# The pool band of a hybrid decoder trunk: the rows of the tile above, packed by a DMA for two matmuls instead of eight

## The chip, the cores and the metric

One core of one Trainium2 chip runs the whole program. The metric is the device time of one execution in microseconds (us); for the kernel before there are three such times, and their median is used. The profile is of one execution.

## The reference, cut to what matters

Two layers over 1024 positions of 1024 channels in float32. The first mixes tokens by trailing means over 2, 4, 8 or 16 positions (one window for each group of 256 channels), minus the token itself, followed by a 256x256 product in each group; the second is a sliding-window attention. Each layer then has a SwiGLU part and an embedding part.

```
hn = rms_norm(h, mix_pre_g[i])
for g, w in enumerate((2, 4, 8, 16)):
    pooled[g] = (cs[t] - cs[t - w]) / min(t + 1, w) - hn[g]       # cs: cumulative sum over positions
y = einsum('bsgc,gcd->bsgd', pooled, w_pool) * pool_scale
h = h + rms_norm(y, mix_post_g[i])
h = h + rms_norm(swiglu(rms_norm(h, ffn_pre_g[i])), ffn_post_g[i])
```

## The kernel before, in words

The 1024 positions are eight tiles of 128. The normed tile t lies in `pool_xn[t % 2]` with its positions on the partitions. `pool_band` turns a tile and takes its trailing means at once: for each of the eight blocks of 128 channels it multiplies the block by a constant band matrix (`band_inner`, L631). The first positions of a tile also need up to 15 positions of the tile above, so behind each of these eight matmuls comes one with 16 columns, which reads the block of the tile above in `pool_xn[1 - p]` and the constant `band_before` (L633). All are float32, and each shows as two MATMUL records. The result fills PSUM banks 0 and 1, which there are only once: the next band waits until ScalarE has taken the high part (`slot_hi`, L395) and VectorE the low part (`slot_lo`, L399).

Each engine runs a list of parts in written order (`staggered`). In step t the parts are these. TensorE: band(t+1), the turn of tile t-2 for the SwiGLU part (`fn_turn`, L517), products(t) (24 matmuls, L315 to L317). VectorE: `add_post(t-1)` (L472 and L475, adds the tile's output to H), `pool_normed(t+2)` (L371), `slot_lo(t+1)` (L399), `fn_normed(t-1)` (L506), `fn_lo(t-2)` (L552). ScalarE: `slot_hi(t+1)`, the squares of tile t+3 (L645), the raw copies of tile t-2 (L533), the squares of H for tile t-1 (L492), the squares of products(t) (L594), the cuts of tile t-2 (L543). GpSimd turns sums of squares into scales (L364, L366; L498, L500). Products(t) go to banks 2+3 or 4+5 by parity. `pool_normed(t+2)` writes the buffer of tile t, and so waits until band(t+1), which still reads it, has ended.

The SyncE queue issues loads in written order: the eight tiles of x, the constants, the pool weights, `sinks`, and then in `ffn_loads(0)` three weight loads of the SwiGLU part (A11, A12, A21), followed by `spill_tile(0..4)`, each of which waits for `add_post` of its tile (`added`). Behind them are the other weight loads. The semaphores of the p loads are four, one for each layer and parity.

Of the kernel before, what the change touches and what calls it, by code (L numbers as in the profile page):

```python
# [22 lines left out]
P = 128  # L23
F32 = mybir.dt.float32
# [6 lines left out]
D = 1024  # L31
SEQ = 1024
TILES = SEQ // P
PAIRS = TILES // 2
KD = D // P
HALF = 512
# [5 lines left out]
LONGEST = max(WINDOWS)  # L42
# [14 lines left out]
def constants():  # L57

    s, t = np.arange(P)[:, None], np.arange(P)[None, :]
    first, inner, before = [], [], []  # L60
    for w in WINDOWS:
        near = (t >= s) & (t - s < w)
        first.append(near / np.minimum(t + 1, w).astype(np.float32) - (s == t))
        inner.append(near / np.float32(w) - (s == t))
        before.append(((t + P - s < w) / np.float32(w))[:, :LONGEST])
    inv = (1.0 / (10000.0 ** (np.arange(0, HEAD, 2, dtype=np.float32) / np.float32(HEAD)))).astype(np.float32)
    angle = np.arange(SEQ, dtype=np.float32)[:, None] * inv[None, :]
    angle = angle.reshape(TILES, P, HEAD // 2).transpose(1, 0, 2)
    q, k = np.arange(P)[:, None], np.arange(-P, P)[None, :]
    valid = (q - k >= 0) & (q - k < P)  # L70
    mask = np.stack([np.where(valid & (k >= 0), 0.0, NEG), np.where(valid, 0.0, NEG)], axis=1)
    out = {
        "identity": np.eye(P),
        "band_first": np.stack(first, 1), "band_inner": np.stack(inner, 1), "band_before": np.stack(before, 1),
        "rope_cos": np.cos(angle), "rope_sin": np.sin(angle),
        "mask_unit": np.concatenate([mask[:, 0], mask[:, 1], np.zeros((P, D - 4 * P))], axis=1),
    }
    return {k: np.ascontiguousarray(v, dtype=np.float32) for k, v in out.items()}
# [12 lines left out]
def trunk(nc, I, out):  # L91
    ctx = ExitStack()
    with ctx:
        credited = []

        def sem(name):
            return ctx.enter_context(nc.semaphore(name))
# [54 lines left out]
        def at(kib, *tensors):  # L152
# [8 lines left out]
        Z = region("Z", 186 * KIB,  # L161

                   at(0, *[(f"raw{i}", [P, D], F32) for i in range(SLOTS)], ("xn0", [P, D], F32), ("xn1", [P, D], F32),
                      ("tmp", [P, D], F32)),

                   at(0, ("b11_hi", PIECES, F32R), ("b11_lo", PIECES, F32R), ("t3_lo", PIECES, F32R)),
                   at(16, ("t3_raw", PIECES, F32)),
                   at(24, ("a11_hi", FORM, F32R), ("a11_lo", FORM, F32R), ("a12_hi", FORM, F32R), ("a12_lo", FORM, F32R),
                      ("m7", [P, HALF], F32), ("d_s4_hi", [P, 2 * P], F32R), ("d_s4_lo", [P, 2 * P], F32R),
# [22 lines left out]
                   at(96, ("late_junk", [P, D], F32)), at(28, ("ffn_junk", [P, D], F32)),  # L192

                   at(36, *weights("w_pool", [P, KD, GROUP]), ("band_first", [P, 4, P], F32), ("band_inner", [P, 4, P], F32),
                      ("band_before", [P, 4, LONGEST], F32), ("scale_row", [P, D], F32), ("pool_gain", [P, D], F32),
                      ("squares", [P, 2, D], F32), ("pool_xn0", [P, D], F32), ("pool_xn1", [P, D], F32),
                      ("pool_raw0", [P, D], F32), ("pool_raw1", [P, D], F32)),
                   at(92, ("pool_junk", [P, 2, D], F32)),
# [18 lines left out]
        A = B = DD = E = Z  # L217
        raw = [Z[f"raw{i}"] for i in range(SLOTS)]
        pool_raw, pool_xn = [Z["pool_raw0"], Z["pool_raw1"]], [Z["pool_xn0"], Z["pool_xn1"]]
        xn, tmp = [Z["xn0"], Z["xn1"]], Z["tmp"]  # L220
        xt_hi, xt_lo = [DD["xt0_hi"], DD["xt1_hi"]], [DD["xt0_lo"], DD["xt1_lo"]]
        post_gain = E["post_gain"]
# [17 lines left out]
        ps = ctx.enter_context(nc.psum_tensor("ps", [P, 8, HALF], F32))  # L240
# [79 lines left out]
        consts_loaded = sem("consts_loaded")  # L320
        first_consts_loaded = sem("first_consts_loaded")
        pool_consts_loaded = sem("pool_consts_loaded")
        w_pool_scaled = sem("w_pool_scaled")
        x_loaded = [sem(f"x_loaded{t}") for t in range(TILES)]
        gain_loaded = sem("gain_loaded")
# [17 lines left out]
        def moved(count):  # L343
            return 16 + 32 * count

        p_loaded = [[sem(f"p_loaded{L}{p}") for p in range(2)] for L in range(2)]
        stored = sem("stored")


# [269 lines left out]
        def pool_band(pe, i, p):  # L619

            s = s_pool
            first = isinstance(i, int) and i == 0 and p == 0
            if isinstance(i, int) and i == 0 and p == 1:
                pe.wait_ge(pool_consts_loaded, 48)
            pe.wait_ge(s["xn"][p], s.done("xn", i))
            t_banks_read(pe, s, i, p)
            for c in range(KD):
                w = c // 2
                band = B["band_first"] if first else B["band_inner"]
                o = banks(0)[:, c * P:(c + 1) * P]  # L630
                last = pe.matmul(o, pool_xn[p][:, c * P:(c + 1) * P], band[:, w, :], start=True, stop=first)  # L631
                if not first:
                    last = pe.matmul(o[:, 0:LONGEST], pool_xn[1 - p][:, c * P:(c + 1) * P], B["band_before"][:, w, :],  # L633
                                     start=False, stop=True)
            last.then_inc(s["turned"][p], 1)
            if first:

                for w in range(12):
                    pe.matmul(ps[:, 6, 0:P], B["band_first"][:, w % 4, :], B["band_first"][:, w % 4, :], start=True, stop=True)
# [143 lines left out]
        def ffn_load(sp, name, source, L, g, t):  # L783

            w = I["w_ff_gate" if source[1] == "1" else "w_ff_up"][L].rearrange("(k p) n -> p k n", p=P)
            k = 4 * (int(source[2]) - 1)
            sp.dma_start(W_RAW[name][:, :, :], w[:, k:k + 4, bass.ds(g * GROUP + t * P, P)]
                         ).then_inc(F["form_loaded"][name], 16)
# [668 lines left out]
        def p_load(sp, L, i, p):  # L1457
            s = S[f"ple{L}"]
            sp.wait_ge(s["p_lo"][p], s.free("p_lo", i))
            sp.dma_start(p_raw[p][:, :, :], I["pT"][L].rearrange("(k c) t -> c k t", c=P)[:, :, bass.ds((2 * i + p) * P, P)]  # L1460
                         ).then_inc(p_loaded[L][p], 16)

        def p_hi(act, L, i, p):
            s = S[f"ple{L}"]
            act.wait_ge(p_loaded[L][p], 16 * i + 16)
            act.wait_ge(s["used"][p], s.free("used", i))
            act.activation(pT[p][0][:, :, :], p_raw[p][:, :, :], ACT.Copy).then_inc(s["p_hi"][p], 1)

# [322 lines left out]
        def _(sp):  # L1791
# [6 lines left out]
            sp.dma_start(B["band_first"][:, :, :], I["band_first"]).then_inc(first_consts_loaded, 16)  # L1798
            w = I["pool_w"][0].rearrange("g c n -> (g c) n")
            x_load(1)  # L1800
            for name in ("band_inner", "band_before"):
                sp.dma_start(B[name][:, :, :], I[name]).then_inc(pool_consts_loaded, 16)
            sp.dma_start(ident[:, :], I["identity"]).then_inc(pool_consts_loaded, 16)
            row_load(sp, B["scale_row"], I["pool_scale"][0], pool_raw_loaded[0])
# [3 lines left out]
            for t in range(3, TILES):  # L1808
                x_load(t)
            sp.dma_start(sinks[:, :], I["sinks"][0].partition_broadcast(P)).then_inc(consts_loaded, 16)  # L1810

            def ffn_loads(L):
                s = S[("pool", "o")[L]]

                def spill_tile(j):
                    sp.wait_ge(s["added"][j % 2], s.done("added", j // 2))
                    sp.dma_start(spill[L][:, j * D:(j + 1) * D], H[:, j * D:(j + 1) * D]).then_inc(F["spilled"], 16)

                first = (0, 0)
                if L == 1:  # L1820
                    sp.wait_ge(s["used"][0], s.done("used", 0))
                ffn_load(sp, "A11", "a11", L, *first)
                ffn_load(sp, "A12", "a12", L, *first)
                if L == 1:
                    sp.wait_ge(*summed("S4", 0, GROUPS - 1, 1))
                ffn_load(sp, "A21", "a21", L, *first)
                for j in range(5):
                    spill_tile(j)
                if L == 1:
                    sp.wait_ge(s["lo"][0], s.done("lo", PAIRS - 1))  # L1830
                ffn_load(sp, "S2", "a22", L, *first)
                sp.wait_ge(s["used"][0], s.done("used", PAIRS - 1))
                ffn_load(sp, "S3", "a11", L, *first)
                ffn_load(sp, "S1", "a22", L, *first)
                spill_tile(5)
                spill_tile(6)
                sp.wait_ge(FN["ssum"], done(TILES * L + TILES - 1))
                ffn_load(sp, "A22", "a22", L, *first)
                spill_tile(TILES - 1)
                ffn_load(sp, "S4", "a12", L, *first)  # L1840
                ffn_load_down(sp, L, 0)
                for t in range(2):
                    ffn_load_tile(sp, L, 0, t)
                with sp.Fori(1, GROUPS - 1) as g:
                    for t in range(2):
                        ffn_load_tile(sp, L, g, t)
                for t in range(2):
                    ffn_load_tile(sp, L, GROUPS - 1, t)
# [601 lines left out]
```

## Time and profile before

| | |
|---|---|
| time of three executions | 1977.02, 1977.14, 1977.79 us; median 1977.14 us |
| span of the profiled execution | 1974.5 us; its own time isn't given apart, the median is 2.6 us above the span |
| TensorE matmul busy | 1923.7 us (97%) |
| VectorE busy | 1410.7 us (71%) |
| ScalarE busy | 897.2 us (45%) |
| GpSimd busy | 457.6 us (23%) |
| the chain that ended last | PE 86%, DVE 8%, POOL 2%, issue 2% |
| pool stage | band(0) starts at 9.64 us, band(7) at 65.55 us, its last products at 74 to 77 us |

In the profile PE is TensorE's matmuls, DVE is VectorE, ACT ScalarE, POOL GpSimd, SPq the queue of SyncE. PEclk is the granted share of TensorE's full clock. A row of a timeline gives start, duration, engine, line, operation, tiles written and read, and in brackets the idle time before it.

### The profile page before, as it was taken

How to read it: one execution, taken by the hardware profiler on the slowest of the kernel's cores; microseconds unless marked ns; L12 is line 12 of the kernel's file. 1: busy time of each engine (PE TensorE's matmuls, PEld its weight loads, DVE VectorE, ACT ScalarE, POOL GpSimd, SP SyncE). 2: the span in 40 equal slices, each digit the busy share in tenths (PEclk: the TensorE clock that was granted, in tenths of full speed). 3: DMA queues.
4: the chain of work that ended last, by engine and by line, in shares of the span. 5: the costliest groups of instructions: out<-in, count | busy, mean ns of one | idle time of the engine just before them, and what ended most of it. 6: DMA issues, size and time to landing. Idle time of an engine off the chain costs nothing.

```text
span 1974.5 us, 28696 instructions
## 1 busy us (share of the span) xinstructions
PE 1923.7 (97%) x9198; PEld 1578.6 (80%) x9198; DVE 1410.7 (71%) x2384; ACT 897.2 (45%) x1726; POOL 457.6 (23%) x448
## 2 busy tenths in 40 slices
PE   7899999999999999999999999999999999999998
PEld 7778888888888878888866687888888888888787
DVE  6887777777777786565478658777777777777863
ACT  5654444444444454341178545444444444444531
POOL 3211222212122221010046211222122221222310
PEclk9999999999999999999999999999999999999999
DMA  5333323233333350254200113233332323235201
GB/s 210 107 97 96 92 82 97 75 102 94 98 94 92 89 203 24 78 221 168 85 12 1 60 48 114 79 101 96 96 95 86 90 74 106 90 105 178 96 29 68
DMA packets 221159, 189.02 MB, mean 96 GB/s; under 512 B 11168, under 2 KB 198944, under 8 KB 221088
## 3 DMA queue, kind: packets, MB, share of 16 engines
q1 hardware_dynamic: 217712, 183.38, 29.0%
q10 hardware_dynamic: 3376, 4.73, 0.7%
q8 instruction: 40, 0.66, 0.1%
q14 instruction: 31, 0.25, 0.0%
HBM read 167.10 MB, written 20.97 MB: 95 GB/s over the span
## 4 chain that ended last, share of the span: by engine, by line
PE 86%; DVE 8%; POOL 2%; issue 2%; ACT 1%; DMA 1%; DVEq 0%; ACTq 0%; POOLq 0%
PE ps L825 14%; PE ps L827 14%; PE ps L826 14%; PE ps L315 7%; PE ps L317 7%; PE ps L316 7%; PE ps L922 7%; PE ps L924 7%; PE ps L923 7%; POOL probs L1679 1%; DVE ps L1644 1%; PE ps L388 1%; PE ps L1633 1%; PE ps L1687 1%; PE ps L631 1%
## 5 line engine op out<-in xcount | busy, mean ns | idle before, releaser
L1247 DVE TENSOR_TENSOR H<-H,ps 128x512 f32<-128x512 f32 x496 | 327.9, 686 | 112.9 <-PE ps L924 112.0
L1109 POOL TENSOR_TENSOR s_raw<-s_raw,a_raw 128x512 f32<-128x512 f32 x66 | 87.5, 1327 | 765.6 <-DVE s_lo L1160 649.3
L825 PE MATMUL ps<-t_hi,s_hi 128*128 128x512 f32 x528 | 206.3, 391 | 6.8 <-DVE t_lo L1259 3.9
L827 PE MATMUL ps<-t_hi,s_lo 128*128 128x512 f32 x528 | 205.5, 389 | 0.0
L826 PE MATMUL ps<-t_lo,s_hi 128*128 128x512 f32 x528 | 205.5, 389 | 0.0
L998 ACT ACTIVATE m<-ps 128x512 f32<-128x512 f32 x44 | 26.4, 599 | 264.9 <-PE ps L827 262.6
L825 PE MATMUL ps<-b_hi,a_hi 128*128 128x512 f32 x352 | 137.7, 391 | 0.0
L826 PE MATMUL ps<-b_lo,a_hi 128*128 128x512 f32 x352 | 137.5, 391 | 0.0
L827 PE MATMUL ps<-b_hi,a_lo 128*128 128x512 f32 x352 | 137.4, 390 | 0.0
L924 PE MATMUL ps<-wd_hi,d_ab_lo 128*128 128x512 f32 x336 | 130.7, 389 | 0.0
L922 PE MATMUL ps<-wd_hi,d_ab_hi 128*128 128x512 f32 x336 | 130.7, 389 | 0.0
L923 PE MATMUL ps<-wd_lo,d_ab_hi 128*128 128x512 f32 x336 | 130.7, 389 | 0.0
L825 PEld LDWEIGHTS ps<-t_hi,s_hi 128*128 128x128 f32 x528 | 99.1, 188 | 29.9 <-DVE t_lo L1259 5.3
L827 PEld LDWEIGHTS ps<-t_hi,s_lo 128*128 128x128 f32 x528 | 99.1, 188 | 20.8
L826 PEld LDWEIGHTS ps<-t_lo,s_hi 128*128 128x128 f32 x528 | 99.1, 188 | 20.4
L976 ACT ACTIVATE s_hi<-s_raw 128x512 fp32r<-128x512 f32 x132 | 82.8, 627 | 54.8 <-DVE s_raw L1109 54.8
L1160 POOL TENSOR_TENSOR a_lo<-a_raw,a_hi 128x512 fp32r<-128x512 f32 x60 | 80.9, 1348 | 114.7 <-ACT a_hi L976 114.7
L315 PE MATMUL ps<-w_ple_gate_hi,xt_hi 128*128 128x512 f32 x256 | 101.7, 397 | 1.6 <-DVE w_ple_gate_lo L291 0.8
L317 PE MATMUL ps<-w_ple_gate_hi,xt_lo 128*128 128x512 f32 x256 | 100.0, 390 | 0.0
L316 PE MATMUL ps<-w_ple_gate_lo,xt_hi 128*128 128x512 f32 x256 | 99.6, 389 | 0.0
L1679 POOL TENSOR_TENSOR probs<-probs,recip 128x1024 f32<-128x1024 f32 x32 | 60.6, 1893 | 153.3 <-DVE recip L1671 153.3
L939 ACT ACTIVATE ps<-ps 128x512 f32<-128x512 f32 x88 | 51.2, 582 | 98.0 <-PE ps L924 90.8
(293 smaller groups left out, 5033.6 us busy)
## 6 DMA issues: line engine op xcount, KB each, us to landing
a_raw<-in_w_ff_gate SPq DMA_DIRECT2D x88, 256.0 KB, 2.9
a_raw<-in_w_ff_up SPq DMA_DIRECT2D x88, 256.0 KB, 3.0
s_raw<-in_w_ff_up SPq DMA_DIRECT2D x88, 256.0 KB, 2.9
s_raw<-in_w_ff_gate SPq DMA_DIRECT2D x88, 256.0 KB, 3.1
wd_raw<-in_w_ff_down SPq DMA_DIRECT2D x44, 512.0 KB, 4.3
residual_spill<-H SPq DMA_DIRECT2D x16, 512.0 KB, 2.6
raw<-in_w_ple_gate SPq DMA_DIRECT2D x16, 512.0 KB, 6.0
back<-residual_spill SPq DMA_DIRECT2D x16, 512.0 KB, 5.3
```

The lines of the kernel that those rows point to most:

```text
L315: pe.matmul(out_, lhs[0], rhs[0], start=first, stop=False)
L316: pe.matmul(out_, lhs[0], rhs[1], start=False, stop=False)
L317: return pe.matmul(out_, lhs[1], rhs[0], start=False, stop=last)
L825: pe.matmul(ps[:, bank, :], w[0], x[0], start=fresh and k == 0, stop=False, skip_group_check=not fresh)
L826: pe.matmul(ps[:, bank, :], w[0], x[1], start=False, stop=False, skip_group_check=not fresh)
L827: last = pe.matmul(ps[:, bank, :], w[1], x[0], start=False, stop=k == 3, skip_group_check=not fresh)
L922: pe.matmul(ps[:, bank, :], a[0], wd_hi[:, b, :], start=fresh, stop=False, skip_group_check=not fresh)
L923: pe.matmul(ps[:, bank, :], a[0], wd_lo[:, b, :], start=False, stop=False, skip_group_check=not fresh)
L924: pe.matmul(ps[:, bank, :], a[1], wd_hi[:, b, :], start=False, stop=True, skip_group_check=not fresh).then_inc(F["down"], 1)
L976: act.activation(W[name][0][:, :, :], form_raw(name), ACT.Copy).then_inc(F["form_hi"], 1)
L1109: eng.tensor_tensor(form_raw(name), W_RAW[name][:, :, :], form_raw(other) if other != "A21" else W_RAW["A21"][:, :, :], op).then_inc(summe ...
L1247: dve.tensor_tensor(dst, dst, src, ALU.add).then_inc(F["summed"], 1)
```

## The change: what it does

The eight matmuls of 16 columns go. Instead SyncE copies the last sixteen rows of each normed tile (16 partitions of 1024 values) into a tile `halo[t % 2]` of 128 partitions by 128 values: row r, channel block c lands on partition 8r + c. A constant `band_halo`, of two blocks of 64 columns, picks from it by channel block, so two matmuls of 64 columns (one for each bank) add all eight corrections. They stand behind the eight inner matmuls and wait for the copy. The copies of tiles 0, 1 and 2 stand in the SyncE queue behind the load A21, the copy of tile j+3 behind the spill of tile j. The semaphores of the p loads become two, with counts that run on over the layers; `band_before` (32 KB) gives way to `band_halo` (64 KB).

```diff
+    halo = np.zeros((P, 2, HALF // KD), np.float32)
+    for c in range(KD):
+        at_ = (c % 4) * LONGEST
+        halo[c::KD, c // 4, at_:at_ + LONGEST] = before[c // 2]
...
-                last = pe.matmul(o, pool_xn[p][:, c * P:(c + 1) * P], band[:, w, :], start=True, stop=first)
-                if not first:
-                    last = pe.matmul(o[:, 0:LONGEST], pool_xn[1 - p][:, c * P:(c + 1) * P], B["band_before"][:, w, :],
-                                     start=False, stop=True)
+                last = pe.matmul(o, pool_xn[p][:, c * P:(c + 1) * P], band[:, w, :], start=first or c % 4 == 0, stop=True,
+                                 skip_group_check=not first and c % 4 > 0)
+            if not first:
+                pe.wait_ge(halo_loaded[1 - p], 16 * (i + p))
+                for b in range(2):
+                    o = ps[:, b, :].rearrange("p (c t) -> p c t", c=4)[:, :, 0:LONGEST]
+                    last = pe.matmul(o, halo[1 - p][:, :], B["band_halo"][:, b, :].rearrange("p (c t) -> p c t", c=4),
+                                     start=False, stop=True, skip_group_check=True)
             last.then_inc(s["turned"][p], 1)
...
-            act.wait_ge(p_loaded[L][p], 16 * i + 16)
+            act.wait_ge(p_loaded[p], 16 * (L * PAIRS + i) + 16)
...
+            def halo_move(t):
+                i, p = t // 2, t % 2
+                sp.wait_ge(s_pool["xn"][p], s_pool.done("xn", i))
+                sp.dma_start(halo[p][:, :], pool_xn[p][P - LONGEST:, :]).then_inc(halo_loaded[p], 16)
...
                 ffn_load(sp, "A21", "a21", L, *first)
+                if L == 0:
+                    for t in range(3):
+                        halo_move(t)
                 for j in range(5):
                     spill_tile(j)
+                    if L == 0 and j + 3 < TILES - 1:
+                        halo_move(j + 3)
```

## Rows read from the trace of the kernel before

**Rows 1.** Stretches of 50 us: busy time of each engine, granted clock, DMA share, GB/s

```profile
50.00:100.00 50.00, 41.53 (x279) 37.71 (x278) 43.85 (x49) 31.86 (x52) 15.04 (x24) 0.92 0.30 106
...
150.00:200.00 50.00, 50.00 (x222) 41.42 (x221) 35.93 (x59) 23.07 (x41) 9.48 (x8) 1.00 0.32 96
```

**Rows 2.** Timeline of TensorE, band(1), products(0) and the start of band(2)

```profile
16.31 0.46 PE L631 MATMUL ps<-band_inner,pool_xn 128*128 128x128 f32 x2
...
16.61 0.29 PE L633 MATMUL ps<-band_before,pool_xn 128*128 128x16 f32 x2
...
16.75 0.47 PE L631 MATMUL ps<-band_inner,pool_xn 128*128 128x128 f32 x2
...
19.88 0.36 PE L315 MATMUL ps<-w_pool_hi,xt_hi 128*128 128x256 f32 x1
...
22.83 0.39 PE L631 MATMUL ps<-band_inner,pool_xn 128*128 128x128 f32 x2
```

**Rows 3.** Timeline of TensorE, band(0) and the twelve matmuls behind it

```profile
9.64 3.75 PE L631 MATMUL ps<-band_first,pool_xn 128*128 128x128 f32 x16 [9.64 <-DVE pool_xn L371]
...
13.19 3.20 PE L639 MATMUL ps<-band_first 128*128 128x128 f32 x24
```

**Rows 4.** Timeline of the SyncE queue: issues, their start and how long they took

```profile
9.84 0.43 SPq L1810 DMA_DIRECT2D sinks_row<-in_sinks  x1
10.32 4.56 SPq L787 DMA_DIRECT2D a_raw<-in_w_ff_gate  x2
14.92 5.93 SPq L787 DMA_DIRECT2D a_raw<-in_w_ff_up  x1
```

**Rows 5.** DMA issues of short stretches: KB each, us from issue to landing

```profile
sinks_row<-in_sinks SPq DMA_DIRECT2D x1, 8.0 KB, 14.7
...
a_raw<-in_w_ff_up SPq DMA_DIRECT2D x1, 256.0 KB, 12.8
...
residual_spill<-H SPq DMA_DIRECT2D x1, 512.0 KB, 2.6
```

**Rows 6.** Stretches of 1 us, and TensorE's timeline, around the fall of the clock

```profile
48.00:49.00 1.00, 1.00 (x8) 1.00 (x6) 1.00 (x3) 0.00 (x0) 0.60 (x1) 0.54 0.00 0
...
54.00:55.00 1.00, 1.00 (x7) 1.00 (x6) 0.26 (x1) 1.00 (x3) 0.71 (x2) 0.55 0.00 0
...
49.65 0.45 PE L633 MATMUL ps<-band_before,pool_xn 128*128 128x16 f32 x2
49.94 0.78 PE L631 MATMUL ps<-band_inner,pool_xn 128*128 128x128 f32 x2
```

**Rows 7.** Timeline of TensorE: starts of bands 3 to 7, ends of 3 and 7

```profile
30.20 0.46 PE L631 MATMUL ps<-band_inner,pool_xn 128*128 128x128 f32 x2 [0.76 <-DVE xt_lo L399]
...
33.76 1.07 PE L517 MATMUL ps<-ident,tmp 128*128 128x128 f32 x8
...
37.56 0.46 PE L631 MATMUL ps<-band_inner,pool_xn 128*128 128x128 f32 x2
...
46.37 0.46 PE L631 MATMUL ps<-band_inner,pool_xn 128*128 128x128 f32 x2 [1.32 <-DVE xt_lo L399]
...
56.94 0.39 PE L631 MATMUL ps<-band_inner,pool_xn 128*128 128x128 f32 x2
...
65.55 0.46 PE L631 MATMUL ps<-band_inner,pool_xn 128*128 128x128 f32 x2 [1.18 <-DVE xt_lo L399]
...
69.12 1.07 PE L517 MATMUL ps<-ident,tmp 128*128 128x128 f32 x8
```

**Rows 8.** Timeline of VectorE and ScalarE: four rows on the way from band to band

```profile
26.50 1.22 DVE L475 TENSOR_TENSOR H<-H,ps 128x1024 f32<-128x1024 f32 x1
28.47 1.05 ACT L492 ACTIVATE pool_junk<-H 128x1024 f32<-128x1024 f32 x1
38.95 1.28 DVE L506 SCALAR_TENSOR_TENSOR tmp<-H,small,gain 128x1024 f32<-128x1024 f32 x1 [1.53 <-POOL small L500]
70.36 1.22 DVE L399 TENSOR_TENSOR xt_lo<-ps,xt_hi 128x1024 fp32r<-128x1024 f32 x1 [1.27 <-ACT xt_hi L395]
```

More of the change, by code:

```diff
@@ L64, in constants @@
         inner.append(near / np.float32(w) - (s == t))
-        before.append(((t + P - s < w) / np.float32(w))[:, :LONGEST])
+        before.append(((t + P - s < w) / np.float32(w))[P - LONGEST:, :LONGEST])
+    halo = np.zeros((P, 2, HALF // KD), np.float32)
+    for c in range(KD):
+        at_ = (c % 4) * LONGEST
+        halo[c::KD, c // 4, at_:at_ + LONGEST] = before[c // 2]
     inv = (1.0 / (10000.0 ** (np.arange(0, HEAD, 2, dtype=np.float32) / np.float32(HEAD)))).astype(np.float32)
@@ L73, in constants @@
         "identity": np.eye(P),
-        "band_first": np.stack(first, 1), "band_inner": np.stack(inner, 1), "band_before": np.stack(before, 1),
+        "band_first": np.stack(first, 1), "band_inner": np.stack(inner, 1), "band_halo": halo,
         "rope_cos": np.cos(angle), "rope_sin": np.sin(angle),
@@ L194, in trunk @@
                    at(36, *weights("w_pool", [P, KD, GROUP]), ("band_first", [P, 4, P], F32), ("band_inner", [P, 4, P], F32),
-                      ("band_before", [P, 4, LONGEST], F32), ("scale_row", [P, D], F32), ("pool_gain", [P, D], F32),
+                      ("band_halo", [P, 2, HALF // KD], F32), ("halo0", [P, P], F32), ("halo1", [P, P], F32), ("scale_row", [P, D], F32), ("pool_gain", [P, D], F32),
                       ("squares", [P, 2, D], F32), ("pool_xn0", [P, D], F32), ("pool_xn1", [P, D], F32),
@@ L219, in trunk @@
         pool_raw, pool_xn = [Z["pool_raw0"], Z["pool_raw1"]], [Z["pool_xn0"], Z["pool_xn1"]]
+        halo = [Z["halo0"], Z["halo1"]]
         xn, tmp = [Z["xn0"], Z["xn1"]], Z["tmp"]
@@ L322, in trunk @@
         pool_consts_loaded = sem("pool_consts_loaded")
+        halo_loaded = [sem(f"halo_loaded{p}") for p in range(2)]
         w_pool_scaled = sem("w_pool_scaled")
@@ L344, in moved @@
             return 16 + 32 * count
-        p_loaded = [[sem(f"p_loaded{L}{p}") for p in range(2)] for L in range(2)]
+        p_loaded = [sem(f"p_loaded{p}") for p in range(2)]
         stored = sem("stored")
@@ L1460, in p_load @@
             sp.dma_start(p_raw[p][:, :, :], I["pT"][L].rearrange("(k c) t -> c k t", c=P)[:, :, bass.ds((2 * i + p) * P, P)]
-                         ).then_inc(p_loaded[L][p], 16)
+                         ).then_inc(p_loaded[p], 16)
         def p_hi(act, L, i, p):
             s = S[f"ple{L}"]
-            act.wait_ge(p_loaded[L][p], 16 * i + 16)
+            act.wait_ge(p_loaded[p], 16 * (L * PAIRS + i) + 16)
             act.wait_ge(s["used"][p], s.free("used", i))
@@ L1800, in _ @@
             x_load(1)
-            for name in ("band_inner", "band_before"):
+            for name in ("band_inner", "band_halo"):
                 sp.dma_start(B[name][:, :, :], I[name]).then_inc(pool_consts_loaded, 16)
```

## The prediction

> **What bounds the kernel now.** I first cut the span into stretches of 50 us. From 100 us on nearly every stretch has TensorE busy throughout at the full clock; the stretch 150 to 200 stands for them. The pool stage is different: 50 to 100 has TensorE at 41.5 of 50 us, VectorE at 43.9 and a mean granted clock of 0.92 [rows 1]. So nothing overlaps the pool stage, and a microsecond that it gets longer or shorter reaches the end. Next I followed the chain of waits through it: it passes in turn through bands, products, GpSimd's scales and, most of the time, VectorE. Band(3), band(5) and band(7) each start when `slot_lo` releases the banks (0.76, 1.32 and 1.18 us of idle TensorE), while band(2), band(4) and band(6) follow the products without a gap [rows 2, 7]. Last I read the SyncE queue beside the DMA landings, since the change adds a transfer there.
>
> **The matmuls.** An inner matmul and its 16-column one start 0.44 us apart from the next pair (16.31 to 16.75), 0.14 of it for the 16 columns (16.61 to 16.75) [rows 2]. A band is 3.56 us (30.20 to 33.76) [rows 7]. Inner matmuls alone go at 0.26 each: 24 records, 12 matmuls, 13.19 to 16.31 [rows 2, 3]. Eight of them take 2.1 us. The two matmuls of 64 columns have no row; by columns they lie between 0.14 (16 columns) and 0.26 (128), I take 0.2, in the middle, 0.4 for both. A band becomes 2.5 us: 1.05 less (bounds 0.95 to 1.2), where the clock is full. At the half clock a 16-column matmul takes 0.29 (49.65 to 49.94) [rows 6].
>
> **The wait of band(1).** This is what decides. The copy of tile 0 stands in the SyncE queue behind A21. The issue of A21 begins at 14.92 and takes 5.93 us, so the copy can't be issued before 20.85 [rows 4]. Band(1) starts at 16.31, its inner matmuls would be done by 18.4, and before it was over at 19.85, just ahead of products(0) at 19.88 [rows 2]. Nor is it there at 20.85: `sinks_row`, 8 KB, was issued at 9.84 and landed 14.7 us later, at 24.5, since it stood behind the loads ahead of it; A21 lands 12.8 us after 14.92, at 27.7 [rows 4, 5]. I put the copy of tile 0 behind A21: 28.0, with 0.3 for its own 64 KB, the copy of tile 1 beside it and the 32 KB more of constants. Bounds: 23.5, if it passes the queue (issue at 20.85 and 2.6 us, what a spill takes with an empty queue [rows 5]), and 29.5. I take 28.0, since the sinks row is the nearest one. The other copies have cover: that of tile 1 lands beside the first and is wanted seven microseconds later; those of tiles 2 to 6 are issued as soon as VectorE has written the tile, a whole step (7 us) before their band ends, and land some 3 us later [rows 5]. The spill in front of each, and the load S2 behind them, wait for events that come no later than now.
>
> The Trainium skill ("DMA: Bandwidth & Descriptors", section Anatomy of one DMA) gives about 2.0 us plus bytes over 436 GB/s per DMA for another queue kind; for 64 KB that is 2.15 us, and the copy would be there at 23.0. By that the sum below would be about 5 us less. The sinks row speaks against using it here.
>
> **Queued behind the waiting matmul** on TensorE are products(0), band(2) and everything after. `slot_hi(1)`, `pool_normed(2)` and the squares behind them wait for band(1) too. So no engine can run ahead.
>
> The sum, by the starts of bands, before and after:
> - 1 to 2: before 6.5 us (16.31 to 22.83). After: TensorE idles from 18.4 to 28.1, then runs two halo matmuls at the half clock (0.6 us), band(1) is over at 28.8 (+8.95). Products(0) follow. 24 matmuls took 2.95 us, 0.12 each [rows 2]. After a long idle time TensorE runs at half pace, 1.2 of 2.4 GHz: band(0), after 9.6 us of idle time, took 3.55 us for eight matmuls, 0.44 each against 0.26 at 13.19 [rows 3]; and when the granted clock fell near 48.1 it came back near 54.9 [rows 6]. So half pace lasts 3.5 to 6.8 us; I take 4.5: until 32.6 there are 18 products at 0.21, then six at 0.12. Band(2) starts at 33.45: **+10.6**.
> - 2 to 3: band(3) waits for a chain from the end of products(0) (squares, scale, `add_post(0)`, `pool_normed(3)`, `slot_lo(2)`), 22.83 to 30.20, which has no band in it: **0**.
> - 3 to 4: before, the products and `slot_lo(3)` were ready together. After, TensorE is free 1.05 us earlier and `slot_lo` sets it. ScalarE started on H of tile 0 at 28.47, 0.75 us after VectorE had written it (27.72), as it was behind with band(2)'s share [rows 8]; band(2) ends earlier against this, so most of this goes: **-0.65**.
> - 4 to 5: `fn_normed(1)` starts 5.2 us after the end of band(3) (33.76 to 38.95, by way of ScalarE and GpSimd), and band(5) 7.4 us after that [rows 7, 8]. After: band(3) 40.8 to 43.3, `fn_normed(1)` 48.5, band(5) 55.9, band(4) having started at 47.5; 8.4 in place of 8.8: **-0.4**.
> - 5 to 6: before 10.57 us, because the clock fell (0.54 in 48 to 49, back in 54 to 55) with band(5), a turn and most of products(4) in it [rows 6, 7]. After, without the fall, VectorE's full step sets it, 7.4 us: **-3.2**.
> - 6 to 7: before 8.6. After: band(5) ends at 58.4, `fn_normed(3)` 5.2 later at 63.6, band(7) 7.4 later at 71.0, against 63.3 for band(6): 7.7: **-0.9**.
> - Behind band(7), `slot_lo(7)` waited 1.27 us for ScalarE, which waited for the band [rows 8]: **-1.05**. From there on VectorE is the bound, and TensorE from 100 us on.
> The sum is +4.4 us. The profiled execution's time is not given apart from its span of 1974.5; the median lies 2.6 above, and I add the difference to the median: 1977.1 + 4.4 = **1981.5 us**. The shared semaphore of the p loads counts the same loads in the same order, and costs nothing.
>
> Why I take no fall of the clock: before the fall at 48.1 TensorE had idled 1.32 us and run a band half of whose matmuls had 16 columns; after idle times of 1.18 (before 65.55) and 0.76 it did not fall [rows 7]. The new band is denser, though idle times of about 1.5 us a step come with it.
>
> **The rivals.**
> - A second fall of the clock, as before, in steps 3 to 7. For it: more idle time in each step. Against it: the denser band. Price: band(5) about 1 us longer, the turn 0.8, products(4) 1.8, of which VectorE's slack swallows about 1: +2.7, 1984.2 us. Chance 0.32.
> - The other side: the copy of tile 0 overtakes the loads. If it lands at 23.5 then band(1) is over 4.5 us earlier, the sum is -0.1 or so: 1977.0, not slower. The point from which it decides is a landing at 23.6. For it: a transfer with an empty queue needs 2.6 us. Against it: the sinks row. This is also where the rule of the Trainium skill leads. Chance 0.10. To be faster by more than 0.2% it would need in addition a short half-pace stretch and the earlier landing of everything behind.
> - The bands gain less than counted (the halo matmuls or the switch between bank patterns cost what the 16-column ones did): the wait remains, and -1.05 and the smaller gains go: +6.5, 1983.6. Against it: the contiguous pace in [rows 3]. Chance 0.06.
> - The forecast: 0.52, its own range 1979.5 to 1983.5 (landing within 1 us, half pace 3.5 to 6.8 us).
>
> **How the numbers follow.** 0.2% is 4 us, about what this kernel's times can tell from no change; the forecast lies just beyond it, at +4.4, so it gives 0.28 to slower, 0.22 to same and 0.02 to faster. The fall of the clock gives 0.31 to slower, the smaller gain 0.05; the rest of both is same. The overtaking copy gives 0.07 to same and 0.03 to faster. Together slower 0.64, same 0.31, faster 0.05. The range, 1977.8 to 1986.0, leaves out most of the overtaking case below and a fall of the clock together with a late landing above.
>
> **What would show it.** TensorE idle for 9 to 10 us inside band(1), ended by a DMA into halo; the copy of tile 0 landing just behind A21, near 28; half-pace products(0); no wait at the halo matmuls of bands 2 to 7; bands of 2.5 us; and band(7) at about 71. Wrong: a copy that lands before 24, a band longer than 2.7 us at the full clock, a second fall of the clock, or a halo wait in a later band.

## The result: 4.8 us slower, and the profile after

The kernel before has a median of 1976.29 us (10 executions, 1974.33 to 1977.79), the changed one 1981.11 us (10, 1980.18 to 1982.63). The ratio is 1.0028, 95% interval 1.0020 to 1.0037: 4 to 7 us slower, beyond what can be told from no change. The forecast was +4.4 us and 1981.5. The profiled execution of the changed kernel took 1980.64 us with a span of 1978.5, 4.0 more than the span before.

Stretches of 50 us of the changed kernel, as in [rows 1], with the first one in front:

```profile
0.00:50.00 50.00, 28.54 (x202) 27.87 (x203) 23.45 (x20) 21.03 (x33) 12.64 (x28) 0.90 0.60 204
50.00:100.00 50.00, 38.93 (x287) 35.84 (x285) 48.90 (x55) 34.85 (x59) 20.09 (x30) 0.97 0.33 113
...
150.00:200.00 50.00, 50.00 (x222) 41.43 (x221) 36.95 (x60) 20.64 (x37) 9.48 (x8) 1.00 0.32 95
```

From 150 us on TensorE is busy throughout in both kernels. VectorE now works 48.9 of the 50 us that follow the first 50 (43.9 before): in this execution it is VectorE that bounds the stage.

The SyncE queue of the changed kernel, the row of A21 and the first copies (compare [rows 4]); then the DMA issues of 14 to 22 us, KB each and us to landing (compare [rows 5]):

```profile
15.03 5.93 SPq L797 DMA_DIRECT2D a_raw<-in_w_ff_up  x1
21.00 9.37 SPq L1826 DMA_DIRECT2D halo<-pool_xn  x3
```

```profile
a_raw<-in_w_ff_up SPq DMA_DIRECT2D x1, 256.0 KB, 12.1
halo<-pool_xn SPq DMA_DIRECT2D x2, 64.0 KB, 6.0
```

A21 lands at 15.03 + 12.1 = 27.1. The first copy, issued at 21.00, ends the wait at 27.3. The chain of waits from 24 to 32 us says what follows:

```profile
21.00 6.31 DMA halo<-pool_xn
27.32 0.04 issue
27.36 1.12 PE ps L643 x4
28.48 0.32 PE ps L320
28.80 0.21 PE ps L321
29.01 0.21 PE ps L322
```

TensorE's timeline, band(1) to the start of band(7) (compare [rows 2, 7]); L637 are the eight inner matmuls of a band, L643 its two halo matmuls:

```profile
16.46 2.02 PE L637 MATMUL ps<-band_inner,pool_xn 128*128 128x128 f32 x16 [0.30 <-DVE xt_lo L405]
27.36 1.12 PE L643 MATMUL ps<-band_halo,halo 128*128 128x64 f32 x4 [8.88 <-DMA halo<-pool_xn]
28.24 0.56 PE L320 MATMUL ps<-w_pool_hi,xt_hi 128*128 128x256 f32 x1
...
33.50 2.09 PE L637 MATMUL ps<-band_inner,pool_xn 128*128 128x128 f32 x16
35.43 0.56 PE L643 MATMUL ps<-band_halo,halo 128*128 128x64 f32 x4
...
40.91 2.02 PE L637 MATMUL ps<-band_inner,pool_xn 128*128 128x128 f32 x16 [1.99 <-DVE xt_lo L405]
42.77 0.56 PE L643 MATMUL ps<-band_halo,halo 128*128 128x64 f32 x4
43.16 1.05 PE L523 MATMUL ps<-ident,tmp 128*128 128x128 f32 x8
...
47.60 2.02 PE L637 MATMUL ps<-band_inner,pool_xn 128*128 128x128 f32 x16 [0.53 <-DVE xt_lo L405]
...
55.78 2.02 PE L637 MATMUL ps<-band_inner,pool_xn 128*128 128x128 f32 x16 [2.01 <-DVE xt_lo L405]
...
62.97 2.02 PE L637 MATMUL ps<-band_inner,pool_xn 128*128 128x128 f32 x16 [1.01 <-DVE xt_lo L405]
...
70.66 2.02 PE L637 MATMUL ps<-band_inner,pool_xn 128*128 128x128 f32 x16 [1.53 <-DVE xt_lo L405]
```

TensorE stands for 8.88 us in the middle of band(1), runs the two halo matmuls and all 24 products(0) at the half clock (28.24 to 33.50, 0.21 each), and from then on a band takes 2.25 us (40.91 to 43.16) instead of 3.56. No later band waits at its halo matmuls; bands 3 to 7 now each wait in front, for VectorE. Up to band(7) the clock doesn't fall again; behind it there is one more fall, which the kernel before has too (0.58 in 85 to 89):

```profile
88.00:92.00 4.00, 3.60 (x13) 3.24 (x14) 3.85 (x5) 1.59 (x3) 0.00 (x0) 0.57 0.00 0
```

### The profile page after: what moved, and what is told of

Same layout as the page of the kernel before. It is cut to its first block, busy times and chain, and to the rows that moved or that the text cites. A ratio compares the mean times of both kernels' runs of the same rounds, so it can differ in the third digit from the quotient of the medians.

```text
span 1978.5 us, 28535 instructions
## 1 busy us (share of the span) xinstructions
PE 1912.9 (97%) x9114; PEld 1567.7 (79%) x9114; DVE 1411.2 (71%) x2384; ACT 898.0 (45%) x1726; POOL 461.7 (23%) x448
## 4 chain that ended last, share of the span: by engine, by line
PE 85%; DVE 8%; POOL 2%; issue 2%; DMA 1%; ACT 1%; SPq 1%; DVEq 0%; ACTq 0%; POOLq 0%
PE ps L835 14%; PE ps L837 13%; PE ps L836 13%; PE ps L320 7%; PE ps L322 7%; PE ps L321 7%; PE ps L933 7%; PE ps L934 7%; PE ps L932 7%; POOL probs L1689 1%; DVE ps L1654 1%; PE ps L394 1%; PE ps L1643 1%; PE ps L1697 1%; DVE t_lo L1269 1%
## 5 line engine op out<-in xcount | busy, mean ns | idle before, releaser
L835 PEld LDWEIGHTS ps<-t_hi,s_hi 128*128 128x128 f32 x528 | 99.1, 188 | 31.3 <-DVE t_lo L1269 7.1
```

Of the source, the lines that this page charges most:

```text
L835: pe.matmul(ps[:, bank, :], w[0], x[0], start=fresh and k == 0, stop=False, skip_group_check=not fresh)
```

## The experiments

Two theories stood. The first: the whole loss is the wait of band(1) for a copy that lands behind the weight loads, and the denser bands gain some of it back. The rival: the copies or the new matmuls cost by themselves. A third question was the clock, on which one term (-3.2) of the sum rested. All kernels are compared with the kernel before, run on the same chip between them.

**The copies issued early** (`early_copy`):

```diff
             x_load(2)
-            for t in range(3, TILES):
+            x_load(3)
+            for t in range(2):
+                halo_move(t)
+            for t in range(4, TILES):
                 x_load(t)
...
-                    for t in range(3):
+                    for t in range(2, 3):
                         halo_move(t)
```

> The changed kernel with the copies of tiles 0 and 1 issued between the loads of x tiles 3 and 4 instead of behind A21. Theory (the wait of band(1) for a copy that lands behind the weight loads is the whole loss): the copy of tile 0 lands by 17 or 18 us, band(1) ends near 19 instead of 28.3, band(2) starts near 22 instead of 33.5, and what the denser bands gain shows: 6 to 8 us faster than the kernel before, 11 to 12 faster than the changed one, about 1969. Rival 1 (the loss is in the new matmuls or the copies themselves, wherever they stand): at or above the kernel before. Rival 2 (the gain of 3.2 us in steps 5 to 6 is luck of the clock, not the denser band): the granted clock falls in the pool stage again, and it is only 3 to 5 us faster than the kernel before.

Measured: 1973.22 us, ratio 0.9983 (0.9974 to 0.9992), 3.1 us faster than before and 7.9 faster than the changed kernel. The wait is gone and the sign with it: the first theory holds for the loss. The size (6 to 8 us were expected) is that of rival 2. TensorE's timeline:

```profile
18.23 0.56 PE L643 MATMUL ps<-band_halo,halo 128*128 128x64 f32 x4
21.84 2.02 PE L637 MATMUL ps<-band_inner,pool_xn 128*128 128x128 f32 x16
...
29.93 3.49 PE L637 MATMUL ps<-band_inner,pool_xn 128*128 128x128 f32 x16 [2.76 <-DVE xt_lo L405]
33.21 0.76 PE L643 MATMUL ps<-band_halo,halo 128*128 128x64 f32 x4
...
46.44 2.98 PE L637 MATMUL ps<-band_inner,pool_xn 128*128 128x128 f32 x16 [2.13 <-DVE xt_lo L405]
```

Bands 3 and 5 come behind 2.76 and 2.13 us of idle TensorE, and take 3.88 and 3.51 us (29.93 to 33.81, 46.44 to 49.95), since the granted clock went to the half within them:

```profile
30.00:33.00 3.00, 3.00 (x16) 3.00 (x17) 2.26 (x2) 0.00 (x0) 1.57 (x2) 0.54 0.14 19
...
47.00:51.00 4.00, 4.00 (x25) 4.00 (x24) 3.97 (x5) 1.04 (x2) 1.41 (x2) 0.57 0.01 2
```

And `add_post(0)`, which before waited only for its scale, now ended 3.21 us of idle VectorE by a DMA:

```profile
24.90 1.29 DVE L478 SCALAR_TENSOR_TENSOR ps<-ps,small,post_gain 128x1024 f32<-128x1024 f32 x1 [3.21 <-DMA gain<-in_ffn_pre_g]
```

The gain row of the SwiGLU part, loaded on ScalarE's queue, lands at 24.8. Before, `add_post(0)` began at 25.17 and didn't meet it. So step 2 to 3 is 8.1 us, not 7.4: 1.0 us saved in front came to a new wait.

**Only band(1) as before** (`tile1_old`; the copy of tile 0 is left out, and the constant `band_before` is loaded too):

```diff
+                if second:
+                    pe.matmul(o, pool_xn[p][:, c * P:(c + 1) * P], band[:, w, :], start=True, stop=False)
+                    last = pe.matmul(o[:, 0:LONGEST], pool_xn[1 - p][:, c * P:(c + 1) * P], B["band_before"][:, w, :],
+                                     start=False, stop=True)
+                    continue
...
-            if not first:
+            if not first and not second:
```

> The changed kernel, but band(1) takes its rows from the tile above by the eight matmuls of 16 columns as before, so nothing waits for the copy of tile 0, which is left out; bands 2 to 7 are the new ones. Theory (only the copy of tile 0 is late): band(1) ends near 19.9, then as in the run with the early copy but 1 us later: 5 to 7 us faster than the kernel before. Rival (later copies cost too): band(2), which now needs the copy of tile 1 that lands behind A21 near 27.3, waits with its halo matmuls: it would have its inner matmuls done at 25 and idle 2 to 2.5 us, and the gain is 3 to 5 us.

Measured: 1973.16 us, ratio 0.9988 (0.9979 to 0.9997). The rival came out: now band(2) waits, for the copy of tile 1.

```profile
23.09 1.95 PE L644 MATMUL ps<-band_inner,pool_xn 128*128 128x128 f32 x16
28.50 1.12 PE L650 MATMUL ps<-band_halo,halo 128*128 128x64 f32 x4 [3.46 <-DMA halo<-pool_xn]
34.64 2.00 PE L644 MATMUL ps<-band_inner,pool_xn 128*128 128x128 f32 x16
```

In each of the five profiles in which the copies stand behind A21, the one that is waited for came between 27.2 and 28.5 us, whichever band wants it. In the profiled execution the clock doesn't fall between this wait and band(7) (bands 4 to 7 start 7.3 to 7.6 us apart). Why the median is level with that of the early copies in spite of the wait is not shown: the eleven executions lie in two groups, seven at 1972.2 to 1973.5 and four at 1975.2 to 1976.2, and the profiled one (1975.44) is of the upper.

**The copies ahead of the three weight loads, behind the loads of x** (`copy_before_weights`):

```diff
             def ffn_loads(L):
                 s = S[("pool", "o")[L]]
+                if L == 0:
+                    for t in range(2):
+                        halo_move(t)
```

> The changed kernel with the copies of tiles 0 and 1 issued behind the loads of x but ahead of A11, A12 and A21. Theory (the landing sets the end one for one, the copies go in order behind the loads ahead): they land near 24.7, like the sinks row of the kernel before (24.5), 2.7 us earlier than in the changed kernel (27.3); the time falls by 2.5 to 3 us, to about the kernel before plus 2. Rival 1 (what matters is the half-pace stretch, not the landing): less than 1 us. Rival 2 (the copies don't queue behind the loads of x): they land near 13, and the time is that of the run with the early copy.

Measured: 1979.35 us, ratio 1.0015 (1.0006 to 1.0024). The issue of the two copies begins at 10.44; they land 14.1 us after issue (median of the two), the sinks row behind them 14.9 after its own; the halo matmuls start at 25.13, 2.23 us before those of the changed kernel:

```profile
25.13 1.12 PE L643 MATMUL ps<-band_halo,halo 128*128 128x64 f32 x4 [6.22 <-DMA halo<-pool_xn]
30.31 1.95 PE L637 MATMUL ps<-band_inner,pool_xn 128*128 128x128 f32 x16
```

Band(2) starts 3.2 us earlier, but the time falls by only 1.8 us, where 2.5 to 3 were expected. So the copies do come behind the loads that were issued ahead of them; that an earlier landing pays one for one is not shown. The profiled execution's clock fell in bands 5 and 7 (the inner matmuls of band(5) took 3.38 us, not 2.02).

**TensorE kept busy during the wait** (`warm_wait`), thirty matmuls that nobody reads:

```diff
             if not first:
+                if isinstance(i, int) and i == 0 and p == 1:
+                    for w in range(30):
+                        pe.matmul(ps[:, 6, 0:P], B["band_first"][:, w % 4, :], B["band_first"][:, w % 4, :], start=True, stop=True)
                 pe.wait_ge(halo_loaded[1 - p], 16 * (i + p))
```

> The changed kernel with 30 float32 matmuls of 128 columns, whose result nobody reads, between the inner matmuls of band(1) and its wait: TensorE is busy to 26.2 of the 27.3 us. Theory (the half pace after the long idle time costs 2.3 us in products(0) and 0.4 us in the halo matmuls, and they are on the chain): band(2) starts near 31 instead of 33.5, and the time falls by 2.5 us against the changed kernel. Rival (the half pace is hidden by the chain of squares, scale and add_post behind products(0)): less than 0.5 us.

Measured: 1982.61 us, ratio 1.0032 (1.0020 to 1.0045): 6.3 us slower than before, no gain on the changed kernel, where 2.5 us were expected; but the test did not isolate what it should. In its profile the copy came at 28.4 and the idle time was still 2.63 us; products(0) began at the full and went on at the half clock:

```profile
28.36 0.66 PE L646 MATMUL ps<-band_halo,halo 128*128 128x64 f32 x4 [2.63 <-DMA halo<-pool_xn]
33.27 1.95 PE L637 MATMUL ps<-band_inner,pool_xn 128*128 128x128 f32 x16
```

From the halo matmuls to band(2) it is 4.9 us, against 6.1 in the changed kernel: 1.2 us less, set against the later landing (1.0) and a fall of the clock in band(5), whose inner matmuls took 2.78 us. The price of the half pace right after the wait stays at the 2.3 us that the rows give (24 products in 5.26 us, not 2.95); no run with this change confirms it.

**The old matmuls with the new wait** (`old_matmuls_wait`; the copies are made and waited for, not used):

```diff
+                if not first:
+                    if c == KD - 1:
+                        pe.wait_ge(halo_loaded[1 - p], 16 * (i + p))
+                    last = pe.matmul(o[:, 0:LONGEST], pool_xn[1 - p][:, c * P:(c + 1) * P], B["band_before"][:, w, :],
+                                     start=False, stop=True)
```

> The kernel before with its eight matmuls of 16 columns in every band, and with the copies and their waits of the changed kernel: the last 16-column matmul of a band waits for the copy, whose content is not used. Theory (the wait alone costs 8.9 us at the end of band(1) and 10 at the start of band(2); the dense bands give back): 8 to 10 us slower than the kernel before if the clock falls once in steps 3 to 7 as it does there, 5 to 7 if it doesn't. Rival (the wait is cheap, the new matmuls are what costs): within 3 us of before.

Measured: 1983.36 us, ratio 1.0037 (1.0023 to 1.0051), +7.0 us, the upper end of what was expected without a fall in steps 3 to 7. With the early copies this makes a table of four, each as the difference from the kernel before in medians:

| | nothing waits | band(1) waits |
|---|---|---|
| eight matmuls of 16 columns | 0 | +7.0 |
| two matmuls of 64 columns | -3.1 | +4.8 |

The wait costs 7 to 8 us, the new matmuls give 2 to 3. In the profile of this run bands 2 to 7 start at 32.91, 40.28, 47.64, 56.45, 63.81 and 72.62, and the granted clock stays at 1.00 from 33 to 80. It falls later, behind band(7):

```profile
33.00:48.00 15.00, 14.24 (x125) 14.03 (x123) 10.97 (x9) 9.19 (x17) 4.86 (x10) 1.00 0.22 77
48.00:60.00 12.00, 10.70 (x95) 10.52 (x95) 10.85 (x11) 8.25 (x17) 6.34 (x10) 1.00 0.17 53
60.00:72.00 12.00, 11.32 (x99) 11.08 (x97) 10.40 (x11) 9.88 (x17) 4.04 (x8) 1.00 0.24 83
...
97.00:105.00 8.00, 6.57 (x33) 6.57 (x34) 7.65 (x11) 4.10 (x7) 0.00 (x0) 0.57 0.85 294
```

So the fall near 48 can go away without a single dense band, and with the same idle time in front of band(5) as before (1.30 us, against 1.32). It shows in the starts: band(5) is 10.08 us later than in the kernel before, band(7) only 7.07, so the missing fall gave 3.0 back.

**The clock in the kernel before** (`before_fill`): four matmuls that nobody reads behind products(3) and products(5).

```diff
+            def fill(i, p):
+                t = 2 * i + p
+                if t not in (3, 5):
+                    return
+                if t >= 2:
+                    pe.wait_ge(FN["raw"], t)
+                for w in range(4):
+                    pe.matmul(ps[:, 6, 0:P], B["band_first"][:, w % 4, :], B["band_first"][:, w % 4, :], start=True, stop=True)
```

> The kernel before, with four float32 matmuls of 128 columns behind products(3) and behind products(5), written to bank 6 and read by nobody; they fill 1.05 of the 1.32 us of idle TensorE before band(5). It tests the term -3.2 of the prediction (steps 5 to 6, 10.57 to 7.4 us, put down to the fall of the granted clock). Theory (the fall follows the idle time, and it costs VectorE about 3 us through band(5) and products(4)): the clock stays up from 48 to 55, and the kernel is 2 to 3.5 us faster than before. Rival (the step is long for other reasons, or the cost is hidden): within 1 us of before.

Measured: 1974.17 us, ratio 0.9991 (0.9982 to 1.0), 2.2 us less in medians, the interval just touching no change. The single executions say more. Of the 21 of the kernel before on this chip, seven had a mean granted clock of 0.999 or 1.000 and took 1973.4 to 1974.6 us; the other fourteen, at 0.996 to 0.998, took 1975.2 to 1977.4. All eleven with the fill took 1973.2 to 1974.5. So the filled kernel always takes the lower time that the unfilled one takes in a third of its executions, 2.1 us less (median 1974.4 against 1976.5). That the two groups are those without and with the fall near 48 is likely, not shown: both profiles of the kernel before have the fall and a mean of 0.996, none is of the other group, and on the chip of the first runs the groups are less clean (0.998 goes with 1974.0 to 1977.7). Its timeline: the idle time before band(5) is 0.41 us, the band takes 3.57 us instead of 5.27, and band(6) follows 7.37 us after band(5), not 10.57.

```profile
47.01 0.46 PE L631 MATMUL ps<-band_inner,pool_xn 128*128 128x128 f32 x2 [0.41 <-DVE xt_lo L399]
...
50.58 1.07 PE L517 MATMUL ps<-ident,tmp 128*128 128x128 f32 x8
...
54.38 0.46 PE L631 MATMUL ps<-band_inner,pool_xn 128*128 128x128 f32 x2
```

**The same fill with the early copies** (`early_copy_fill`: the kernel `early_copy` with seven matmuls behind products(1), (3) and (5); the diff is against the fill above):

```diff
-                if t not in (3, 5):
+                if t not in (1, 3, 5):
...
-                for w in range(4):
+                for w in range(7):
```

> The kernel with the early copies, plus seven such matmuls (1.8 us) behind products(1), (3) and (5), where its TensorE idled 2.76, 2.13 and 2.17 us; its granted clock fell to the half at 30.3 in band(3) and at 47.6 in band(5), which took 3.9 and 3.5 us instead of 2.25. Theory (that is where the gain of the denser bands went): both bands take 2.3 us, the falls don't come, band(7) starts 2.5 to 3.5 us earlier than 62.7, and the time is near 1970.5, 5.5 to 6.5 us faster than the kernel before. Rival (VectorE sets the pace, a band at the half clock is hidden): within 1 us of the run without the fill, 1973.

Measured: 1970.20 us (1969.18 to 1970.46), ratio 0.9971 (0.9959 to 0.9982): 6.2 us faster than before, as expected, and the best version that computes the whole result. No band is slow and band(7) starts at 59.79, 2.9 us before that of the run without the fill:

```profile
44.91 2.02 PE L637 MATMUL ps<-band_inner,pool_xn 128*128 128x128 f32 x16 [0.36 <-DVE xt_lo L405]
...
59.79 2.02 PE L637 MATMUL ps<-band_inner,pool_xn 128*128 128x128 f32 x16
```

Adding 21 useless matmuls to a TensorE that is 97% busy made the kernel 3 us faster (each of the two versions taken against the kernel before on its own chip).

**No rows from the tile above** (`no_halo`, the changed kernel without its copies, halo matmuls and waits; this leaves out that part of the means):

```diff
-            if not first:
-                pe.wait_ge(halo_loaded[1 - p], 16 * (i + p))
-                for b in range(2):
...
-                    for t in range(3):
-                        halo_move(t)
```

> The changed kernel without the rows of the tile above: no copies, no halo matmuls, no wait. It leaves out that part of the trailing means. It bounds what can be gained by taking work out of the bands. Theory (the copies and the two halo matmuls cost 0.35 to 0.4 us a band and nothing else once the copy is early): 0 to 2 us faster than the run with the early copies, 1971 to 1973. Rival (copies and spills share the queue and delay each other, so the copies cost more): 4 us faster or more.

Measured: 1970.06 us, ratio 0.9971 (0.9961 to 0.9981), 3.2 us less than the early copies: between theory (0 to 2) and rival (4 or more), so neither is confirmed. It is level with the filled version, but it is not the least that the bands could take: in its profile the granted clock was at the half from 30.4 to 33.8, in and behind band(3), as nothing fills its idle times.

**Three kernels profiled again.** They were the changed one, the one with the early copies and the one before, as they stood.

> The changed kernel once more, one look. It tells how much of the band starts is the program and how much the execution. Theory: the copy of tile 0 lands within 1 us of 27.3, band(2) starts within 1 us of 33.5; whether the clock falls in steps 3 to 7 can differ (it did not in the first profile), and then band(7) starts 2 to 3 us later than 70.7. Rival: everything repeats within 0.2 us.

> The kernel with the early copies once more, one look. Theory: band(2) starts within 0.7 us of 21.8; its idle times before bands 3 and 5 are longer than 2 us, so the clock falls again in or behind at least one of them, and band(7) starts between 60 and 63.5. Rival: no fall at all, band(7) near 60.

> The kernel before once more, one look. Theory: the clock falls again near 48 behind the idle time before band(5), since all bands start as in the first profile within 0.7 us. Rival: it does not fall, band(7) starts near 62, and the 10.57 us of step 5 to 6 were this one execution's.

Measured, one execution each: 1982.34, 1971.31 and 1976.76 us. The changed kernel's halo matmuls start at 27.50 (27.36 the first time), band(2) at 32.66, but now the clock falls in band(5) and in band(7):

```profile
54.90 3.43 PE L637 MATMUL ps<-band_inner,pool_xn 128*128 128x128 f32 x16 [1.94 <-DVE xt_lo L405]
...
71.40 2.92 PE L637 MATMUL ps<-band_inner,pool_xn 128*128 128x128 f32 x16 [2.12 <-DVE xt_lo L405]
74.12 0.95 PE L643 MATMUL ps<-band_halo,halo 128*128 128x64 f32 x4
```

Band(7) starts only 0.7 us later than in the first profile, not 2 to 3, because the half pace behind the wait ended earlier and band(2) started 0.84 us earlier; band(4) was still 0.8 earlier (46.80 against 47.60), so a shorter half-pace stretch is not hidden by the chain behind it. With the early copies the clock falls once up to band(7) (between 31 and 35), not twice, and band(7) starts at 61.17 in place of 62.68; that execution took 2.3 us less. In the kernel before it falls again near 48, behind 1.39 us of idle time. The wait is the program's; which bands meet the half clock is in part the execution's.

## Why the prediction was right

The mechanism of the loss was right: where TensorE waits, for what, and for how long. That the whole number agrees to 0.4 us is in part luck, since one term rests on a reason that the runs contradict.

By the starts of bands, predicted and measured:

| | predicted | measured | the execution before |
|---|---|---|---|
| copy of tile 0 there | 28.0 | 27.3 | |
| band(1) over | 28.8 | 28.2 | 19.85 |
| band(2) | 33.45 | 33.50 | 22.83 |
| band(3) | 40.8 | 40.91 | 30.20 |
| band(4) | 47.5 | 47.60 | 37.56 |
| band(5) | 55.9 | 55.78 | 46.37 |
| band(6) | 63.3 | 62.97 | 56.94 |
| band(7) | 71.0 | 70.66 | 65.55 |
| end of the program | +4.4 | +4.0 span, +4.8 medians | |

- **The wait** was right in place, cause and size: SyncE's A21 issue (5.93 us again), the landing behind A21, everything queued behind one waiting matmul. `copy_before_weights` shows the order of the queue, the table of four shows the price. The rival with a copy at 23.5 us fell: 6.3 us from issue to landing here, against 2.3 for the later copies, which had only a spill ahead of them. For another queue kind the Trainium skill ("DMA: Bandwidth & Descriptors", section Anatomy of one DMA) has a sum by which 64 KB take 2.15 us, an estimate; the 2.3 us of those later copies agree with it, and the 6.3 us of the one that decides do not.
- **The band** came out at 2.25 us where 2.5 was put: the inner matmuls took 1.86 (eight at 0.23, not 0.26), the two halo matmuls 0.39 (0.4 put). That is 1.3 us less than before a band, outside the stated 0.95 to 1.2. The rows of [rows 3] from which 0.26 came begin while the pace was just coming up: single records there are 0.21 us apart until 13.8, and 0.11 after. (The profile's granted clock reads 1.00 all through band(0), so those rows show a slow start but not the half clock itself; in the wait of band(1) it does read 0.50, from 23.6 to 33.8.)
- **Half pace** lasted longer than taken: all 24 products, not 18, so that the stretch from the end of band(1) to band(2) took 5.26 us, not 4.65 (the prediction's own terms, 18 at 0.21 and six at 0.12, give 4.5), within the stated bound of 3.5 to 6.8 us at half pace. The earlier landing (27.3, not 28.0) made up for it, which is luck: the start of band(2) agrees to 0.05 us with two errors in it. In the second profile the half pace ended after 3.8 us (27.5 to 31.3), and band(2) started 0.84 us earlier though the copy came 0.14 later.
- **The -3.2 of step 5 to 6** has the right size for a step without the fall (measured -3.4, and `before_fill` shows 7.37 us where 7.4 was said), but that the fall was absent was luck. The reason given, the denser band, is wrong. `old_matmuls_wait` lost the fall with bands that are not denser, and kernels with dense bands have it: up to band(7), twice with the early copies, twice in `copy_before_weights`, twice in the second profile of the changed kernel, once in the second of the early copies. The rival of a second fall (+2.7, chance 0.32) was therefore no rival but part of the spread: the changed kernel's ten executions lie between 1980.18 and 1982.63, the profiled one without a fall up to band(7) at 1980.64, the second profiled one, with two, at 1982.34. It is also the sign of being wrong that the prediction named, "a second fall of the clock".
- **The other gains** (-0.65, -0.4, -0.9, -1.05, together -3.0) measured -0.67, -0.63, -0.92 and, from the start of band(7) to `slot_lo(7)`, -1.3 (74.17 - 70.66 against 70.36 - 65.55): -3.5. What the new matmuls give in time is 2.2 to 3.1 us by the table of four, less than this. With the early copies the fill shows that the falls take about 3 us; how much they take in the changed kernel no run shows.

So of the +4.4, the wait side was +10.6 (measured 10.7 at band(2)) and the rest a sum whose largest term stood on the clock of single executions. The forecast set an execution of the kernel before with the fall against one of the changed kernel without it. Where the clock falls in both, the change costs more: in the second profiles, with a fall in each, 1982.34 us against 1976.76, or against 1977.79 for another execution of the kernel before on that chip, so 4.6 to 5.6 us, from single executions.

## What to carry to other kernels

A copy that feeds the next step is only as early as the queue it is put in: read the landing of the last small transfer in that queue, not the transfer's own duration, and place the issue ahead of bulk loads that nobody waits for yet. When work is taken out of an engine that then waits for another, look at what its clock does in the gaps: with the early copies half of the gain went there, and 21 useless matmuls (5.2 us) in the gaps brought it back; four of them in each of two gaps helped the kernel before as well, by about 2 us. A term that rests on one execution's clock belongs in the range, not in the sum.

## What the runs showed of the hardware that was not expected

- TensorE's granted clock went from the full to the half (2.4 to 1.2 GHz) in a stage in which it was 71 to 87% busy over the 10 us before, behind idle times of 1.3 to 2.8 us (1.32 in front of band(5) in the kernel before, 2.76 and 2.13 with the early copies), and stayed up after others of the same length (2.01 and 1.53 us in the changed kernel's first profile, 1.30 in `old_matmuls_wait`, 2.51 in the second profile of the early copies). The Trainium skill ("TensorE: Matmul & The Clock Gate", table Why this matters for your kernels) advises to keep idle gaps between bursts of matmuls short and names a length; here gaps shorter than that were followed by falls.
- What a fall costs depends on where it comes: the one near 48 us cost 3.0 us by the starts of bands (`old_matmuls_wait`, above), the one in 85 to 89 us of the kernel before nothing: VectorE's instructions come 2.36 us later there than in `before_fill`, whose granted clock stays at 1.00 up to 110 us, both ahead of it (at 71 us) and behind it (at 98 us).
- A copy of 64 KB from 16 partitions to 128 within SBUF landed 2.3 us after its issue with only a spill ahead of it, 5.8 to 7.3 us behind the three weight loads, 5.6 to 7.5 us behind the loads of x up to tile 3, and 14.1 us behind all loads of x.
- Per matmul of float32 with 128 rows at the full clock: 0.14 us with 16 columns, 0.18 to 0.2 with 64, 0.23 with 128. Eight times the columns took 1.6 times as long, which is why two matmuls of 64 columns (0.36 to 0.41 us) are cheaper than eight of 16 (1.14 us).
